# Sample attention of a hybrid decoder step: pages turned on VectorE, scores in 32-row products, part of the centring on Pool

## The reference

```python
q_lat = einsum('bthd,rhd->bthr', q[..., :64] * g_k[:64], w_uk)      # queries in latent space
def one(pt, ql, qp, cn, kn, sn):                                    # one sample
    c_all  = concat([cache_kv[pt].reshape(L, 256), cn])             # L = 4096 cached tokens, 8 own
    kp_all = concat([cache_kpe[pt].reshape(L, 32), kn])
    ki_all = concat([cache_kinv[pt].reshape(L, 16), sn])
    s = einsum('thr,kr->htk', ql, c_all) + einsum('thr,kr->htk', qp, kp_all)
    s = where(allowed, s * ki_all.T[:, None, :] * SCALE, -inf)
    p = softmax(s)
    o_lat = einsum('htk,kr->thr', p, c_all)
    return einsum('thr,rhd->thd', o_lat, w_uv)
```

## Time and profile before

| | us |
|---|---|
| median of 3 runs | 1610.06 (1608.57 to 1610.48) |
| the profiled execution | 1610.4 |
| its span | 1608.5 |
| stage of the samples, first scores to last own tokens | 351.6 to 677.3 |

### The profile page before, as it was taken

The page is one execution under the profiler, slowest core; times in us unless marked ns, Lnnn a source line. Parts: engine busy times, 40 slices in busy tenths (PEclk is TensorE's granted clock), DMA queues, the critical chain, the costliest instruction groups (busy, mean ns, idle before and its releaser), DMA issues.

```text
span 1608.5 us, 35404 instructions
## 1 busy us (share of the span) xinstructions
PE 1558.9 (97%) x14238; PEld 1154.4 (72%) x14238; DVE 753.2 (47%) x1628; ACT 587.2 (37%) x1412; POOL 237.9 (15%) x304
## 2 busy tenths in 40 slices
PE   6999999999999999998999999999999999999998
PEld 4455566678888888876777777777767677777753
DVE  2154444457444444446565656657565623013422
ACT  3056444454333333253535444363535231210000
POOL 0000230310122212010000000000000025536200
PEclk9999999999999999999999999999999999999999
DMA  9713787712444444421111111111111125343302
GB/s 328 269 53 113 223 229 262 187 49 84 111 116 119 118 118 120 113 57 29 35 51 41 39 41 38 41 52 40 51 29 49 29 55 176 80 140 96 112 4 82
DMA packets 179518, 159.95 MB, mean 99 GB/s; under 512 B 37866, under 2 KB 157674, under 8 KB 178332
## 3 DMA queue, kind: packets, MB, share of 16 engines
q1 hardware_dynamic: 168780, 118.46, 25.6%
q0 software_dynamic: 9648, 36.19, 7.3%
q10 hardware_dynamic: 928, 3.05, 0.5%
HBM read 133.02 MB, written 24.64 MB: 98 GB/s over the span
## 4 chain that ended last, share of the span: by engine, by line
PE 67%; DVE 5%; ACT 4%; DVEq 2%; issue 1%; POOL 0%; ACTq 0%
PE me_bank L2838 12%; PE rw_bank L1653 9%; PE sa_psS L1120 8%; PE sa_psOs L1148 7%; PE me_bank L2858 3%; PE sa_psA L1105 3%; PE rw_bank L1692 2%; DVE rw_gram L2415 2%; PE sa_psS L1117 2%; PE rw_bank L1754 1%; PE rw_bank L1665 1%; PE rw_bank L1678 1%; PE rw_bank L1773 1%; PE rw_bank L1905 1%; PE rw_bank L1825 1%
## 5 line engine op out<-in xcount | busy, mean ns | idle before, releaser
L1653 PE MATMUL rw_bank<-hT,big 128*128 128x288 f32 x672 | 183.0, 417 | 0.8 <-ACT prep L2090 0.7
L1653 PEld LDWEIGHTS rw_bank<-hT,big 128*128 128x128 f32 x672 | 122.0, 190 | 33.1 <-issue 2.3
L1120 PE MATMUL sa_psS<-qlT,sa_cT_pages 128*128 128x128 f32 x1024 | 131.3, 282 | 0.0
L1120 PEld LDWEIGHTS sa_psS<-qlT,sa_cT_pages 128*128 128x128 f32 x1024 | 119.1, 192 | 7.7
L1215 ACT COPY sa_cT_pages<-sa_psA 128x512 f32<-128x512 f32 x128 | 68.7, 589 | 145.7 <-PE sa_psA L1105 145.7
L1262 DVE TENSOR_TENSOR sa_ST<-sa_psS,kinvp 128x512 f32<-128x512 f32 x64 | 44.3, 692 | 151.5 <-PE sa_psS L1120 150.9
L1678 PE MATMUL rw_bank<-hT,big 128*128 128x288 f32 x256 | 73.5, 421 | 0.0
L739 PE MATMUL pr_psZ<-hT,qlT 128*128 128x288 f32 x256 | 73.1, 406 | 0.1
L1451 POOL COPY shc<-prep 128x3 f32<-128x3 f32 x8 | 1.5, 188 | 470.7 <-ACT rw_xs L2118 470.7
L993 POOL DMA_DIRECT2D big<-in_cache_kv x80 | 44.2, 552 | 180.1 <-issue 180.1
L2897 ACT COPY big<-me_bank 128x288 f32<-128x288 f32 x42 | 16.7, 398 | 144.8 <-PE me_bank L2838 141.7
(11 more groups left out here) (541 smaller groups left out, 3247.9 us busy)
## 6 DMA issues: line engine op xcount, KB each, us to landing
big<-in_w_in SPq DMA_DIRECT2D x44, 512.0 KB, 4.2
big<-in_cache_kv POOLq DMA_DIRECT2D x80, 128.0 KB, 2.9
pages<-in_cache_kv POOLq DMA_DIRECT2D x80, 128.0 KB, 2.7
fr_wada<-in_w_ada SPq DMA_DIRECT2D x8, 1024.0 KB, 11.6
qk_scratch<-oaT SPq DMA_DIRECT2D x32, 192.0 KB, 2.6
big<-in_cache_kv SPq DMA_DIRECT2D x48, 128.0 KB, 2.7
pages<-in_cache_kv SPq DMA_DIRECT2D x48, 128.0 KB, 2.7
fr_wada<-in_w_ada SPq DMA_DIRECT2D x2, 2048.0 KB, 10.3
```

What stands on the lines that cost most here:

```text
L1120: last = nc.tensor.matmul(psS[:, c, 0:ROW], cT[:, g % 2, r, c * P:(c + 1) * P], M.qlT[:, r, n, :, :].rearrange("p h t -> p (h t)"), start= ...
L1653: last = mm(bank[h][:, 0:HT], w[:, ORDER[q], k, :], M.hT[:, k, (F0, F1)[h]], start=(k == 0), stop=(k == KT - 1))
```

## The change

- **Turning.** VectorE turns the latents itself, as 32x32 blocks (`latents_by_blocks`), one instruction of 128x1024 a group from SBUF to SBUF, and kpe in two halves a sample (`keys_by_blocks`). TensorE's `transposes` and `key_transposes` and ScalarE's copies are gone.
- **Scores.** A block keeps the 32 tokens of a page quarter apart, so the products have 32 rows: for each of 8 blocks of the latent and each of 4 row bands one product, plus four for kpe: 36 products a group. Queries are the stationary operand and stand on the partitions of the result, and lie four times, once in each row band (q4). For that they go to DRAM (`store_queries`) and back (`load_queries`), four DMAs of 128 KB a sample.
- **Back to the keys.** ScalarE copies psS to S (`scores_to_sbuf`), TensorE turns it by four transpositions (`scores_to_keys`) into psT (two buffers), and `weighted_scores` reads psT.
- **Own tokens** of all samples are computed once, ahead of the loop, in two halves of 512 columns.
- **Centring.** VectorE centres the own tokens and two chunks of 4 pages, Pool three chunks of 8 pages (`centre_on_pool`). The prompt's gates move from VectorE to Pool.
- **Output.** ScalarE copies psO to olr (`output_raw`) and VectorE divides from there. LAG is 3. SP loads groups 0, 2, 4, 6, 7 of a sample and Pool 1, 3, 5.

The core of the diff:

```diff
-        LAG = 2
-        CHUNKS = ((0, 4), (4, 8), (8, 16), (16, 24), (24, 32))
+        LAG = 3
+        CHUNKS = ((0, 1), (1, 2), (2, 4), (4, 6), (6, 8))
+        BY_DVE, BY_POOL = 2, 3
...
+        def centre_on_pool(pool, s, c):
+            pool.wait_ge(top_taken, s + 1)
+            part, (a, b) = part_of(s, c), CHUNKS[c]
+            nc.gpsimd.tensor_tensor(part, part, bc(topB[:, :], GP * (b - a), 1), ALU.subtract).then_inc(centred_pool, 1)
...
+            for hp in range(NP):
+                M.gate_prompt(pool, hp)
+            for n in range(1, BD):
+                for g in range(G):
+                    for c in {2: (2,), 3: (3,), 4: (4,)}.get(g, ()):
+                        centre_on_pool(pool, n - 1, c)
+                    done = G * n + g - (G + LAG)
...
+            def load_queries(s):
+                for b in range(GP):
+                    sp.dma_start(q4[s % 2][rows_of(b), :, :], M.q_dram[:, :, s, :]).then_inc(q_in[s % 2], 16)
...
+            sp.wait_ge(M.absorb_ev, 4)
+            store_queries(slice(0, 1))
+            sp.wait_ge(q_out, 16 * GP)
+            load_queries(0)
+            store_queries(slice(1, BD))
...
+            def scores(i):
+                n, g = i // G, i % G
+                pe.wait_ge(cT_sb, i + 1)
+                if g % 4 == 0:
+                    pe.wait_ge(kT_sb, 2 * n + g // 4 + 1)
                 if g == 0:
-                    pe.wait_ge(kT_sb, n + 1)
-                else:
-                    pe.wait_ge(cT_sb, G * n + g)
+                    pe.wait_ge(q_in[n % 2], 16 * GP * (n // 2 + 1))
+                if i >= 1:
+                    pe.wait_ge(copied, i)
+                for b in range(GP):
+                    rows = rows_of(b)
+                    nc.tensor.matmul(psS[:, b, 0:ROW], M.qpT[rows, n, :, :].rearrange("p h t -> p (h t)"), kT[rows, g, :], start=True, stop=False)
+                for a in range(NCB):
+                    for b in range(GP):
+                        rows = rows_of(b)
+                        done = nc.tensor.matmul(psS[:, b, 0:ROW], q4[n % 2][rows, a, :], cT[rows, g % 2, a, :], start=False, stop=(a == NCB - 1))
+                done.then_inc(scored, 1)
+
+            def scores_to_keys(i):
+                pe.wait_ge(copied, i + 1)
+                pe.wait_ge(weighted, i + 1)
                 for c in range(GP):
+                    done = nc.tensor.transpose(psT[i % 2][:, c * P:(c + 1) * P], S[:, i % 2, c * P:(c + 1) * P], M.ident[:, :])
+                done.then_inc(turned, 1)
...
+            own_tokens()
+            for i in range(ALL):
+                n, g = i // G, i % G
+                scores(i)
+                if i > 0:
+                    scores_to_keys(i - 1)
+                if n >= 1 and g == 2:
+                    top_to_columns(n - 1)
+                if n >= 2 and g == LAG + 1:
+                    latents_to_columns(n - 2)
+                if i >= G + LAG:
+                    weights_times_latents((i - G - LAG) // G, (i - G - LAG) % G)
+                if n >= 1 and g == 1:
+                    top_to_rows(n - 1)
...
+            for i in range(ALL):
+                n, g = i // G, i % G
+                scores_to_sbuf(i)
+                if n == 0 and g > 0 and g + 1 < NP:
+                    M.gate_sigmoid(act, g + 1)
+                if n >= 2 and g == LAG:
+                    output_raw(n - 2)
+                if n >= 2 and g == LAG + 2:
+                    output_to_sbuf(n - 2)
+                if n >= 1:
+                    for c in {2: (0, 1), 3: (2,), 4: (3,), 6: (4,)}.get(g, ()):
+                        exponentials(n - 1, c)
...
+            for i in range(ALL):
+                n, g = i // G, i % G
+                if i > 0:
+                    weighted_scores(i - 1)
+                if n >= 1 and g == 1:
+                    keys_by_blocks(n, 1)
+                if g == 5 and n + 1 < BD:
+                    keys_by_blocks(n + 1, 0)
+                if i + 2 < ALL:
+                    latents_by_blocks(i + 2)
+                if n >= 1 and g == 1:
+                    spread_top(n - 1)
+                    for c in range(BY_DVE):
+                        centre(n - 1, c)
+                if n >= 2 and g == LAG:
+                    output(n - 2)
+            weighted_scores(ALL - 1)
```

## The result

The changed kernel takes 1597.97 us (median of 4 runs, 1595.94 to 1599.31) against 1610.27 us of the kernel before in the same session: a ratio of 0.9924, 95% interval 0.9907 to 0.9941. It is 12.3 us faster; the prediction had 1620 us, slower. The profiled execution has a span of 1596.0 us, 12.5 us under the 1608.5 of before.

A forecast was written before the change was run, and what follows sets the result against it. TensorE was taken as the bound, busy 1558.9 of 1608.5 us. To 1610.4 us came +2.3 (start, samples, one more group of weights, last exponential) and +8 for the clock: 1620.7, rounded to 1620 us; range 1586 to 1642.

The forecast's parts named there:

- TensorE's groups: TensorE's work on four pages: 4.55 us instead of 5.03; a sample bounded only by TensorE takes 37.6 us.
- The rival on packing: Score products: 32-row tiles don't pack as said, a round costs 0.16 us, kernel 1644 us and more; chance 0.08.
- The engines alternate: Centring: VectorE's two-SBUF-operand instructions wait for Pool's, turn by turn; a sample takes 42.0 us.
- Undisturbed: A sample without interference between Pool and VectorE: 38.55 us, of which the raw output copy alone costs 0.9.
- The clock: Clock falls behind TensorE's idle blocks of 3 to 5 us, at the start and in seven samples: 1 us each, +8.
- rival (c): The clock falls in each sample at the full price of 3.5 us: 1637 us and a little more; chance 0.12.
- Samples 0 and 1: First two samples: 25.6 us (eight groups of 3.2) plus 38.8, 64.4 against 72.15 before, -7.7.
- The start: Queries pass through DRAM before the first scores, which come at 360.0, 8.5 us late; bounds 6 and 12.
- Sample 7 and behind: Last sample +3.8 us, one more group of weights behind the loop +1.7, last second exponential +1: +6.5.
- (a): No interference between Pool and VectorE in these shapes: -24 us, kernel 1586 us; chance 0.20.
- rival (b): Pool and VectorE interfere only partly: 2 us lost a sample, kernel 1600 us; chance 0.12.

The follow-up runs named there:

- e_raw: e_dve with ScalarE copying the raw output ahead of the copy of group 3's scores, not behind it: 1581.9 us.
- e_seq: The changed kernel with a group's 32 score products ordered one 32-row tile after the other, not in rounds over four tiles: 2161.4 us, one run.
- e_drain: The changed kernel with a VectorE drain added before each of its two centrings: 1637.9 us.
- e_dve: The changed kernel with all five centrings on VectorE, none on Pool, and the next stage in the order of the kernel before: 1583.7 us.
- e_start: The changed kernel with sample 0's queries stored and loaded over two queues, SP's and ScalarE's, instead of SP's alone: 1597.4 us.
- e_tail: The changed kernel with, in the next stage, sample 6's output scaled ahead of Pool's subtractions, not behind the centrings: 1599.3 us.
- e_late: The changed kernel with Pool's first subtraction waiting until VectorE has done its own tokens' subtraction and both its centrings: 1591.7 us.

## Why the prediction was wrong

**TensorE's groups: right.** 4.55 us a group, exactly as forecast, the last digit by chance: the transpositions took 0.59 instead of 0.44, and the 0.2 us put between the parts did not come; eight groups and what stands once a sample are 37.7 us (37.6 forecast), which e_raw reaches. By the Trainium skill, "TensorE: Matmul & The Clock Gate", Part 3, four 32-row tiles gain a factor of 3.07; by an estimate from it a group would have cost 0.65 us more. These shapes gave 3.6 in e_seq, and the measurement decides. The rival on packing is out: a round costs 0.11 us, and the passes take 0.028 us only in the order that goes round the four tiles.

**The engines alternate: the step that failed.** The prediction read two pairs in the earlier trace rows, both VectorE instructions that stand behind a drain, and made of them that Pool and VectorE take turns, instruction by instruction. What the rows show is that a VectorE instruction on two SBUF operands that comes while Pool's is under way waits for its end. Whether Pool gets in between two VectorE instructions that follow each other directly, no row of before showed. It doesn't: in the change subtraction and both centrings pass in one go, and Pool's second takes 3.6 us, 1.3 more than its own. e_drain makes the forecast's case by two drains, and there it happens. The Trainium skill, "SBUF — State Buffer", section "Who interferes with whom", says that the order of issue decides who is held up. The first half of the collision agrees (2.48 us). For the second the rows don't settle it: Pool's second instruction is recorded from 554.72, VectorE's first centring from 554.83, and it is VectorE's that runs at once; but both records begin before the instruction ahead on the same engine has ended (554.76 and 554.90), so they don't tell which of the two asked first.

This step carried 13.6 us in samples 2 to 6, which were put at 42.0 us and take 39.28; sample 1 was put at 38.8 and takes 36.49, sample 7 at 42.4 and takes 40.0 up to the end of its last scores' transpositions. Undisturbed the forecast had 38.55 and e_dve has 38.11, so what Pool costs a later sample is 1.2 us, not 3.5. The difference of 0.44 is that of ScalarE's output copy, which costs 0.40 and not 0.9.

**The clock: a consequence of the same step.** The prediction charged 8 us for falls behind blocks of 3 to 5 us in seven samples. The waits in samples 1 to 7 are at most 1.80 us and the clock never falls behind them. From the samples' start on it falls there, behind 3.29 us idle, in the next stage behind 2.23 us, and at 887 us, each time for 3.4 us (the last 3 us of the trace apart); the one of 6.8 us at 744 in the kernel before is gone. Nor is every wait of that size followed by a fall: e_start has 2.22 us at 675.16 and the change 2.48 us at 731.70, both with the clock at 1.00 around them, while the same wait as the latter had the fall at 744 behind it. What the fall at the start costs is in the table as part of samples 0 and 1 (3.25 us for 64 passes instead of 1.79). Under the forecast's own condition, though, the charge was too small: e_drain has falls of 3.4 to 10.2 us in all seven samples and is at 1638, which is the price of rival (c), not of the forecast.

**Samples 0 and 1: the sum right by luck, its parts not.** 64.5 us against 64.4, but as 28.0 + 36.5, not 25.6 + 38.8. The chain of the kernel after in sample 0:

```profile
367.33 0.60 PE sa_psT L1162 x4
367.96 0.69 DVE sa_ST L1333
...
370.51 1.23 DVE sa_cT_blocks L1298
```

It runs through the transpositions to the keys and VectorE's weighting and turn, where the prediction had only the scores and ScalarE's copy: groups of 3.1 to 3.8 us, not 3.2, and the first of 4.5 by the clock. Sample 1 without Pool takes 32.9 us (e_dve) and lost 3.6 to it; the prediction walked it to 38.8.

**The start: mechanism right, size off.** +5.9 instead of +8.5. The hops are as forecast, store, land, issue, load. The evacuation ended at 348.8 instead of the 350.0 assumed (the trace is 0.9 us ahead of that of before already at 297 us), the stores land in 1.9 us, not 2.6, and three issues, not four, stand ahead of the landing at either hop (2.0 us, not 2.4).

**Sample 7 and behind: +7.8 against 6.5, near by two errors.** Up to the end of the last scores' transpositions (658.35) sample 7 takes 40.0 us against 38.6 before, +1.4 where the forecast had +3.8. Behind that it is +6.4 where it had +2.7: 1.7 for the extra group of weights, as forecast; 2.9 that are gone in e_dve, from Pool's last centrings and the fall of the clock behind 2.23 us, for which the prediction had 1; the remaining 1.8 stay open. Nowhere did it ask who else on VectorE would wait beside them: a scaling (2.20 instead of 0.35 us) and instructions of 8 and 24 columns (3.83 us in the change, 4.16 in e_tail) did.

**Rivals.** The 1598 us lie within the stated range, but on the other side of the kernel before, to which the prediction gave 0.32. (a), no interference, was priced at 1586; e_dve, which comes nearest to that case (no centring on Pool, but all of it on VectorE), takes 1583.7. The change as it stands is rival (b), 1598 against 1600, with 14 us lost to Pool, 2.0 for each of seven samples as that rival has it, though unevenly (3.6, five times 1.2, 1.5, and 2.9 behind the last). The mechanism of the forecast was real, its arbitration was assumed.

## What to carry to other kernels

Before giving work to Pool, look at what VectorE does in that stretch: here the instructions that read PSUM or turned ran at their usual length, and those with two SBUF operands waited, so that 3.5 us a sample of VectorE's work given away cost it as much in waiting, and the kernel 14 us. Where such a pair can't be avoided, let VectorE's instructions follow each other without a drain, start Pool behind them (e_late, 6 us), and look at every instruction queued behind, also the smallest. Before pricing a contention from two rows, look what stands ahead of them: both were behind a drain, and the case that mattered was not. And test an engine's help by taking it away: here that made the kernel 14 us faster (e_dve).

## What the runs showed of the hardware that was not expected

**Who gets through.** Beside Pool's subtraction: a stream transposition takes 1.23 us as always, a product with one operand in PSUM 0.67; waiting are a tensor_tensor on two SBUF operands, a tensor_scalar (2.20 and 4.16 us) and an SBUF copy. The copy, from the timeline of e_tail:

```profile
673.18 1.55 DVE L2609 COPY prep<-ssT 128x8 f32<-128x8 f32 x1
```

Eight columns, 1.55 us; the same copy takes 3.83 us in the kernel after, beside Pool's third centring and two memsets (675.89). Of the last two kinds no row of before spoke.

**A clock that falls under a busy engine.** In e_seq the clock falls behind the idle time at the start, as in the other kernels, but then stays at 0.50 for 164 us though TensorE has hardly a gap. It rises at 521 us and falls again 3.4 us later with no gap at all; a later sample has 0.64 in the mean. Windows of e_seq:

```profile
437.90:449.40 11.50, 11.50 (x65) 11.28 (x64) 3.11 (x3) 0.00 (x0) 2.58 (x3) 0.50 0.01 1
...
521.10:524.50 3.40, 3.40 (x42) 3.40 (x43) 0.00 (x0) 0.00 (x0) 0.00 (x0) 1.00 0.14 39
524.50:534.70 10.20, 10.20 (x47) 8.89 (x43) 2.54 (x3) 1.54 (x2) 0.00 (x0) 0.50 0.15 40
...
779.92:889.30 109.38, 109.38 (x679) 97.77 (x679) 28.27 (x35) 9.71 (x17) 15.29 (x15) 0.64 0.19 51
```

What the engine did ahead of the fall was 32-row passes on one tile at a time. Ahead of the rise at 521 us stood the first weights times latents, full 128-row products (L1192, from 517.5 on). With the same 32-row passes over four tiles the clock stays at 1.00 [after, windows above]. So idle time is not the only thing behind which the clock falls; which property of the stream it is, was not tried. The granted clock of e_seq is 0.847 in the mean of 2159.6 us, which costs at most 330 us (an estimate), enough for the 240 us by which it is above the 1920 expected.
